# The w_up product of a gated block: activations stationary, and its squared features turned by VectorE

## What is computed

```python
xn = rms_norm(x, norm_mix)
proj = xn @ w_in                       # (256, 2048) @ (2048, 10248)
# branch A: chunkwise mLSTM on part of proj; branch B: MoBA attention on another part
merged = g[..., :D_MODEL] * (h_a @ w_branch_a) + g[..., D_MODEL:] * (h_b @ w_branch_b)
x = x + merged @ w_out
hn = rms_norm(x, norm_mlp)
x = x + jnp.square(jax.nn.relu(hn @ w_up)) @ w_down     # w_up (2048, 8192), w_down (8192, 2048)
```

## Time and profile before

| | |
|---|---|
| median of 3 runs | 1366.26 us (1365.49 to 1367.26) |
| the profiled execution, its own time | 1367.06 us |
| its span, first to last instruction | 1365.2 us |
| TensorE matmul busy | 1359.2 us |
| TensorE weight load busy | 1141.8 us |
| VectorE busy | 835.5 us |
| ScalarE busy | 632.0 us |
| DMA, mean over the span | 190 GB/s |

### The profile page before, as it was taken

The page is one execution under the profiler, slowest core; times in us unless marked ns, Lnnn a source line. Parts: engine busy times, 40 slices in busy tenths (PEclk is TensorE's granted clock), DMA queues, the critical chain, the costliest instruction groups (busy, mean ns, idle before and its releaser), DMA issues.

```text
span 1365.2 us, 17369 instructions
## 1 busy us (share of the span) xinstructions
PE 1359.2 (100%) x6543; PEld 1141.8 (84%) x6543; DVE 835.5 (61%) x989; ACT 632.0 (46%) x777; POOL 15.2 (1%) x35
## 2 busy tenths in 40 slices
PE   9999999999999999999999999999999999999999
PEld 7788888888888888888888888888888888888887
DVE  4778678545675666689865655444445655644443
ACT  4655555464444444444544444333334444434332
POOL 1010000000000000000000000000000000000000
PEclk9999999999999999999999999999999999999999
DMA  8555654555655655555655555555555555555552
GB/s 280 173 197 179 201 175 155 185 160 179 247 185 185 210 185 190 183 200 171 216 189 188 190 193 195 185 188 201 196 185 187 190 190 192 192 189 187 199 198 92
DMA packets 132551, 258.74 MB, mean 190 GB/s; under 512 B 6250, under 2 KB 8340, under 8 KB 132244
## 3 DMA queue, kind: packets, MB, share of 16 engines
q1 hardware_dynamic: 130336, 257.97, 56.7%
q10 hardware_dynamic: 2164, 0.09, 0.1%
HBM read 255.94 MB, written 2.10 MB: 189 GB/s over the span
## 4 chain that ended last, share of the span: by engine, by line
PE 98%; DVE 1%; DMA 0%; issue 0%; ACT 0%; SPq 0%; DVEq 0%; ACTq 0%
PE ps L933 23%; PE ps L935 23%; PE ps L934 23%; PE ps L948 17%; PE ps L952 9%; PE ps L964 1%; DVE w_lo L617 0%; DVE ps L635 0%; DMA rows<-in_x_dram 0%; PE ps L1071 0%; PE ps L984 0%; PE ps L1014 0%; PE ps L1033 0%; PE ps L1034 0%; PE ps L1032 0%
## 5 line engine op out<-in xcount | busy, mean ns | idle before, releaser
L617 DVE TENSOR_TENSOR w_lo<-raw,w_hi 128x1024 fp32r<-128x1024 f32 x480 | 584.9, 1224 | 485.3 <-ACT w_hi L365 483.2
L365 ACT ACTIVATE w_hi<-raw 128x1024 fp32r<-128x1024 f32 x480 | 506.3, 1062 | 639.7 <-PE ps L935 451.6
L948 PE MATMUL ps<-xT,w_hi 128*128 128x512 f32 x1024 | 319.2, 395 | 0.0
L933 PE MATMUL ps<-w_hi,xT 128*128 128x512 f32 x640 | 254.2, 397 | 0.7 <-DVE w_lo L617 0.7
L935 PE MATMUL ps<-w_hi,xT 128*128 128x512 f32 x640 | 249.5, 390 | 0.0
L934 PE MATMUL ps<-w_lo,xT 128*128 128x512 f32 x640 | 249.1, 389 | 0.0
L952 PEld LDWEIGHTS ps<-xT,w_lo 128*128 128x128 f32 x1024 | 190.0, 188 | 43.9
L952 PE MATMUL ps<-xT,w_lo 128*128 128x256 f32 x1024 | 198.9, 278 | 0.0
L948 PEld LDWEIGHTS ps<-xT,w_hi 128*128 128x128 f32 x1024 | 157.2, 189 | 1.4
L933 PE MATMUL ps<-w_hi,merged 128*128 128x512 f32 x384 | 149.5, 389 | 0.2 <-DVE merged L820 0.2
L933 PE MATMUL ps<-w_hi,branch 128*128 128x512 f32 x384 | 149.5, 389 | 0.0
(11 more groups left out here) (174 smaller groups left out, 673.5 us busy)
## 6 DMA issues: line engine op xcount, KB each, us to landing
raw<-in_w_in_dram SPq DMA_DIRECT2D x79, 1024.0 KB, 5.1
raw<-in_w_up_dram SPq DMA_DIRECT2D x64, 1024.0 KB, 5.3
raw<-in_w_down_dram SPq DMA_DIRECT2D x64, 1024.0 KB, 5.0
raw<-in_w_out_dram SPq DMA_DIRECT2D x16, 1024.0 KB, 5.0
raw<-in_w_branch_b_dram SPq DMA_DIRECT2D x8, 1024.0 KB, 5.1
raw<-in_w_branch_a_dram SPq DMA_DIRECT2D x8, 1024.0 KB, 5.0
rows<-in_x_dram SPq DMA_DIRECT2D x8, 256.0 KB, 7.7
rows<-in_x_dram SPq DMA_DIRECT2D x1, 2048.0 KB, 8.1
```

What stands on the lines that cost most here:

```text
L365: act.activation(w_hi[:, k % RING, :, :], raw[:, k // 2, KH * (k % 2):KH * (k % 2) + KH, :], ACT.Copy).then_inc(hi_made, 1)
L617: dve.tensor_tensor(w_lo[:, k % RING, :, :], raw[:, k // 2, KH * (k % 2):KH * (k % 2) + KH, :], w_hi[:, k % RING, :, :].bitcast(F32), ALU. ...
L933: pe.matmul(o, hi, w_hi[:, s, i, :], start=first, stop=False)
L948: return pe.matmul(ps[:, q0 + j, :], w_hi[:, s, i, P * j:P * j + P], xT[:, t, :, :].rearrange("p a c -> p (a c)"), start=t == 0, stop=t == ...
```

## The change

w_up uses `half_rows`, like every other stage, in two banks a block (banks 4, 5 and 6, 7 in turn); `half_cols` is removed. The result has tokens on the partitions, in one sum. ScalarE takes its Relu into SBUF (and frees the banks), squares it, and VectorE turns the square in sixteen 32x32-block transposes into PSUM (banks 0, 1 and 2, 3 in turn), four ahead of each of the splits 14 to 17. ScalarE copies the turned features from PSUM to their hi part ahead of split 18, and VectorE subtracts for the lo part. VectorE's add and product go. The waits of TensorE follow the new banks.

```diff
--- before.py
+++ after.py
@@ -123,8 +123,8 @@
         gate_f = gate[:, :, :, :].rearrange("p a m n -> p (a m n)")
         sq = gate_f[:, 0:1024]
         e_t = gate_f[:, 0:768].rearrange("p (b c) -> p b c", b=2)
-        up_lo = gate_f[:, 0:1024].rearrange("p (j t) -> p j t", j=4)
-        up_sq = gate_f[:, 1024:2048].rearrange("p (j t) -> p j t", j=4)
+        up_pos = gate_f[:, 0:1024]
+        up_sq = gate_f[:, 1024:2048]
         prob = sb("prob", [P, 2, 384])
         probT = sb("probT", [P, 2, 384])
         prob_f = prob[:, :, :].rearrange("p b c -> p (b c)")
@@ -214,8 +214,8 @@
         xr_landed, x2_summed, x2_turned, x2_hi, x2_lo = (
             sem(s) for s in ("xr_landed", "x2_summed", "x2_turned", "x2_hi", "x2_lo"))
 
-        up_kept, up_read, up_squared, up_hi, up_lo_made = (
-            sem(s) for s in ("up_kept", "up_read", "up_squared", "up_hi", "up_lo_made"))
+        up_read, up_squared, up_turned, up_hi, up_lo_made = (
+            sem(s) for s in ("up_read", "up_squared", "up_turned", "up_hi", "up_lo_made"))
         down_m0 = sem("down_m0")
         down_read, stored = sem("down_read"), sem("stored")
         dve_step, pool_step = sem("dve_step"), sem("pool_step")
@@ -583,13 +583,16 @@
                     with act.Fori(0, 2) as jj:
                         for u in range(2):
                             j = 4 * half + 2 * jj + u
-                            q0 = 4 * ((u + 1) % 2)
                             act.wait_ge(w_used, 8 * (blk0 + j) + 8)
-                            act.activation(up_lo, ps[:, q0:q0 + 4, S:2 * S], ACT.Copy).then_inc(up_kept, 1)
+                            act.activation(up_pos, banks(4 + 2 * u, 6 + 2 * u), ACT.Relu).then_inc(up_read, 1)
                             for i in range(12, 20):
-                                if i == 14:
-                                    act.wait_ge(up_squared, 8 * f + j + 1)
-                                    act.activation(feat[:, bass.ds(4 * (2 * jj + u), 4), 0, :], up_sq,
+                                if i == 13:
+                                    act.wait_ge(up_read, 8 * f + j + 1)
+                                    act.activation(up_sq, up_pos, ACT.Square).then_inc(up_squared, 1)
+                                if i == 18:
+                                    act.wait_ge(up_turned, 8 * f + j + 1)
+                                    act.activation(feat[:, bass.ds(4 * (2 * jj + u), 4), 0, :],
+                                                   banks(2 * u, 2 * u + 2).rearrange("p (t c) -> p t c", t=4),
                                                    ACT.Copy).then_inc(up_hi, 1)
                                 split_hi(blk0 + j + i // 8, i % 8)
 
@@ -894,18 +897,23 @@
                     with dve.Fori(0, 2) as jj:
                         for u in range(2):
                             j = 4 * half + 2 * jj + u
-                            q0 = 4 * ((u + 1) % 2)
-                            dve.wait_ge(up_kept, 8 * f + j + 1)
-                            dve.tensor_tensor(up_sq, ps[:, q0:q0 + 4, 0:S], up_lo, ALU.add).then_inc(up_read, 1)
-                            dve.wait_ge(up_read, 8 * f + j + 1)
-                            dve.scalar_tensor_tensor(out=up_sq, in0=up_sq, scalar=0.0, in1=up_sq, op0=ALU.max,
-                                                     op1=ALU.mult).then_inc(up_squared, 1)
+                            turned = banks(2 * u, 2 * u + 2)
+                            squared = up_sq.rearrange("p (m n) -> p m n", m=M)
                             for i in range(12, 20):
                                 if i == 14:
+                                    dve.wait_ge(up_squared, 8 * f + j + 1)
+                                    turn_blocks(turned, squared, 0, 4)
+                                if i == 15:
+                                    turn_blocks(turned, squared, 4, 8)
+                                if i == 16:
+                                    turn_blocks(turned, squared, 8, 12)
+                                if i == 17:
+                                    turn_blocks(turned, squared, 12, 16, up_turned)
+                                if i == 18:
                                     dve.wait_ge(up_hi, 8 * f + j + 1)
                                     ft = feat[:, bass.ds(4 * (2 * jj + u), 4), :, :]
-                                    dve.tensor_tensor(ft[:, :, 1, :], up_sq, ft[:, :, 0, :].bitcast(F32),
-                                                      ALU.subtract).then_inc(up_lo_made, 1)
+                                    dve.tensor_tensor(ft[:, :, 1, :], turned.rearrange("p (t c) -> p t c", t=4),
+                                                      ft[:, :, 0, :].bitcast(F32), ALU.subtract).then_inc(up_lo_made, 1)
                                 split_lo(blk0 + j + i // 8, i % 8)
                 def down_splits(first, last):
                     for i in range(first, last):
@@ -935,27 +943,6 @@
                         last = pe.matmul(o, lo, w_hi[:, s, i, :], start=False, stop=end)
                     if m == 0 and first_done is not None:
                         last.then_inc(first_done, 1)
-                last.then_inc(w_used, 1)
-
-            def half_cols(blk, k, q0):
-
-
-                pe.wait_ge(lo_made, 8 * blk + k + 1)
-                s = k % RING
-
-                def by_hi(j, i):
-                    t = KH * k + i
-                    return pe.matmul(ps[:, q0 + j, :], w_hi[:, s, i, P * j:P * j + P],
-                                     xT[:, t, :, :].rearrange("p a c -> p (a c)"), start=t == 0, stop=t == KT - 1)
-
-                def by_lo(j, i):
-                    return pe.matmul(ps[:, q0 + j, 0:S], w_lo[:, s, i, P * j:P * j + P], xT[:, KH * k + i, 0, :],
-                                     start=False, stop=False)
-
-                for j in range(4):
-                    for part in (by_lo, by_hi) if k == 7 else (by_hi, by_lo):
-                        for i in range(KH):
-                            last = part(j, i)
                 last.then_inc(w_used, 1)
 
             def turn(dst_bank, col, src):
@@ -1126,19 +1113,16 @@
 
                 for j in range(2):
                     if f == 1:
-                        pe.wait_ge(down_read, M * 2 * (j + 1))
-                    elif j == 1:
-                        pe.wait_ge(kept[0], 16)
-                        pe.wait_ge(kept[1], 16)
+                        pe.wait_ge(down_read, M * (j + 1))
                     for k in range(8):
                         if f == 0 and j == 0 and k in (0, 6):
                             pe.wait_ge(x2_lo, 3 + k // 6)
-                        half_cols(blk0 + j, k, 4 * ((j + 1) % 2))
+                        half_rows(blk0 + j, k, 4 + 2 * j, xT, 2 * k, start=k == 0, stop=k == 7)
                 with pe.Fori(1, 4) as jj:
                     for u in range(2):
                         pe.wait_ge(up_read, 8 * f + 2 * jj + u - 1)
                         for k in range(8):
-                            half_cols(blk0 + 2 * jj + u, k, 4 * ((u + 1) % 2))
+                            half_rows(blk0 + 2 * jj + u, k, 4 + 2 * u, xT, 2 * k, start=k == 0, stop=k == 7)
 
                 for pair in range(2):
                     pe.wait_ge(up_read, 8 * f + 7 + pair)
```

## The result

| | before | after |
|---|---|---|
| median of 4 runs | 1365.88 us (1365.27 to 1367.26) | 1357.38 us (1357.08 to 1357.86) |
| profiled execution, its own time | 1367.06 us | 1357.86 us |
| its span | 1365.2 us | 1356.0 us |
| TensorE matmul busy, count | 1359.2 us, 6543 | 1348.3 us, 6031 |

The ratio of the medians is 0.9938, its 95% interval 0.9924 to 0.9952: 8.5 us faster, where 8.7 had been forecast (a time of 1357.6, against 1357.38 measured).

A forecast was written before the change was run, and what follows sets the result against it. It took the number of TensorE matmuls to bound the stage, each costing its columns and some 14 ns. 1367.06 - 8.7 = 1358.4, for the median 1357.6 us, other work hidden; range 1356.0 to 1359.6, extended to 1361.0.

The forecast's parts named there:

- The term of 8.7 us: w_up on TensorE: both passes fall to w_down's 174.09 us, gaining 4.35 and 4.34 us, together 8.7.
- The lower bound of 7.3: w_up on TensorE: four matmuls saved a half block at 14.2 ns each, 4 x 0.0142 x 128 = 7.3 us.
- whatever its width: TensorE: a matmul costs its columns and some 14 ns, independent of how many columns it has.
- The sum: Whole kernel: profiled run 1367.06 - 8.7 = 1358.4 us; for the median, 0.8 lower, 1357.6.
- The stated range: Whole kernel: 1356.0 to 1359.6 us, from gains of 7.3 to 8.7 widened by run spread; extended to 1361.0 for rival 1.
- The rule spoken of against the change: TensorE: the skill's N/2.4 + 2.5 ns a warm matmul would make the gain only an estimated 1.3 us.
- Rival 2: w_up on TensorE: columns alone set the pace, so nothing is gained, 1366.3 us; chance 3%.
- 18.3 us a block: VectorE in w_up: work rises from 13.5 to 18.3 us a block, 84% of 21.76, hidden and costed at nothing.
- The timetable: Queues at w_up's block boundaries: split and turn end times after T; least slack 4.3 us, at lo 17.
- The tight place: w_up's first block, split for k = 6: ends at 672.6, needed at 673.1; holds by 0.5 us.
- Rival 3: w_up: VectorE becomes the bound above 21.76 us a block, slower than before from 22.3; doubled turns give 1419 us; chance 3%.
- Rival 1: w_up's 16 blocks: small TensorE stalls of 0.22 us each give back 3.5 us, 1361.1 us; chance 8%.

The follow-up runs named there:

- rows_320_192: The changed kernel with w_up's third product (lo features by w_hi) issued as two matmuls, of 320 and 192 columns; measured 1377.44 us.
- rows_128: The changed kernel with w_up's third product cut into four matmuls of 128 columns; measured 1476.87 us.
- one_turn: The changed kernel with 15 of the 16 turns of each w_up block left out; measured 1357.32 us.
- turns_20: The changed kernel with 4 more turns a block, one in each group, to a spare buffer; measured 1357.45 us.
- rows_16: The changed kernel with w_up's third product issued as two matmuls of 256 columns, 8 wide and 8 narrow a half block; measured 1365.59 us.
- turns_at_once: The changed kernel with all sixteen turns of a block moved ahead of split 14; measured 1367.52 us.
- cols_wide: The kernel before, with w_lo also multiplied by the activations' lo part: 16 matmuls of 512 columns a half block of w_up, weights stationary; measured 1473.73 us.
- turns_32: The changed kernel with 16 more turns a block, to a spare buffer that nobody reads; measured 1432.85 us.

## Why the prediction was right

**TensorE.** The mechanism is the one forecast: fewer matmuls for the same columns. The term of 8.7 us was measured as 178.44 - 174.08 and 178.43 - 174.08, 8.7. Its working needs two corrections. The cost beside the columns is 13.3 ns a matmul, so four fewer are 4 x 0.0133 x 128 = 6.8 us; the other 1.9 us come from no longer mixing widths. The lower bound of 7.3 took 14.2 ns for a fixed cost and was too high as a bound. And "whatever its width" is wrong below 256 columns (`rows_320_192`, `rows_128`), which the kernel before could not show, since it has nothing narrower than 256.

**The number.** That the time came within 0.2 us of 1357.6 is partly luck. The sum started from 1366.26, the median of three launches; 46 launches of the same kernel beside the experiments have medians of 1365.36 to 1365.58, and from there the sum gives 1356.7 to 1356.9. Two kernels with the changed kernel's w_up passes, `one_turn` and `turns_20`, are at 1357.32 and 1357.45, 8.26 and 8.05 us under the kernel before on their chips. The missing half microsecond has about the size of the longer end of the kernel, which no term of the sum had. The stated range was also mis-added: 8.7 and 7.3 us off 1366.26, widened by the spread of runs, give 1356.8 to 1360.0, not 1356.0 to 1359.6. The measured time lies in both.

**The rule spoken of against the change** (the Trainium skill, TensorE: Matmul & The Clock Gate, Back-to-back issue gap: N/2.4 + 2.5 ns) does not hold here: all forms of one width show 13.3 ns. The section gives that rule for the isolated gap of one matmul; for a stream of weight loads and matmuls, which is what runs here, it gives about 131 ns at N = 512, and the trace shows 227. Rival 2, the columns alone, falls with `rows_16`, where the columns stayed and the gain went.

**VectorE.** 18.3 us a block were counted; the second pass has 136.78 / 8 = 17.1, since the last block's turns fall into w_down. That all of it is hidden is shown by `one_turn`, and by `turns_20` with some to spare.

**The timetable** was right to 0.2 us as far as lo 17; lo 18 came 0.6 late, because the hand-overs to ScalarE and back around the hi copy take 0.4 and 0.3 us (last turn ends at 696.57, copy starts at 696.99) and were counted as nothing. It cost nothing; the least slack became 4.0 us, at lo 18. Used on `turns_at_once` it found the split and the 0.4 us by which it is late, but not that a stall costs 0.13 us more than the delay.

**The tight place** at k = 6 of the first block held: its split ends at 671.5, needed at 655.68 + 16.32 = 672.0.

**Rival 3** was rightly given little, but its edge was mis-sized: "once VectorE needs over 21.76 us a block" took its work alone. With gaps and the wait for the split behind the Relu and Square about 0.9 us must be added, so it decides from about 20.9 us of work; the point from which the change would have been slower than before is under 24 turns' worth (21.95 us, measured 1372), not 22.3. Doubled turns made 1432.85, not 1419. The margin was 2.6 us of work, not 3.5.

**Rival 1** did not occur: TensorE has no wait in w_up, and `one_turn` is no faster.

## What to carry to other kernels

Where TensorE is full, read its pace from the starts at the edges of two stages with the same columns: the difference is the price of the form, and here it carried over to 0.1 us. Give each weight load 512 columns to stream: cutting four of them in two, in each half block, cost the whole gain (`rows_16`), and pieces of 128 columns cost 119 us (`rows_128`). The turning that this form needs is free as long as VectorE's work a block, with the gaps and hand-overs, stays under TensorE's, and as long as it is spread between the splits (the same sixteen turns in one piece cost 10 us, more than the change brings).

## What the runs showed of the hardware

- At the 2.4 GHz level an fp32r matmul with its own weight load costs its columns and 13.3 ns, at 512 and at 256 columns (all of one width); at 512 it does so whichever operand is stationary (`cols_wide`). At the 1.2 GHz level 512 columns took 0.427 us, the columns alone (`turns_32`).
- Pieces of 128 columns between wide matmuls cost 0.115 us each on average, with weight loads 0.11 us apart; a pair of 320 and 192 costs 0.267 us (`rows_128`, `rows_320_192`).
- Mixing widths of 512 and 256 costs 13 to 18 ns a half block more, and hardly depends on how often they alternate (2 or 8 times). The cause is open.
- After a wait of TensorE the second matmul starts 0.33 us after the first instead of 0.23 (`turns_at_once`).
- A transpose of 32x256 fp32 elements in 32x32 blocks takes VectorE 0.456 us from SBUF to PSUM, beside a full TensorE and without slowing it (`one_turn`).
